# Two SBUF start addresses in a two-layer decoder kernel: the rows of y 192 bytes past a multiple of 256, the shared area 64 past one

## The chip, the core and the metric

The kernel runs on one NeuronCore of a Trainium2 chip, with the other cores idle. The metric is device time in microseconds (us). The reference's inputs and outputs are float32, and one launch computes the whole decoder trunk. SBUF is the on-chip memory that every operand of the compute engines is read from; an address here is the byte offset in each of its 128 partitions. TensorE is the matrix engine (PE in the profile, and PEld for its loads of the stationary operand), DVE is VectorE, ACT ScalarE, POOL GpSimd and SP the queue that issues the large DMAs.

## The reference, cut to what matters

```python
D_MODEL, SEQ, FFN_HIDDEN = 1024, 512, 2816
# layer 0
y = rmsnorm(x, g0)
cols = y @ w_in            # mLSTM heads and differential attention heads
x = x + concat(mlstm(cols), diff_attention(cols)) @ w_out
y = rmsnorm(x, g1)
x = x + (silu(y @ w_gate) * (y @ w_up)) @ w_down
# layer 1: the same, with native sparse attention (compressed, selected, window branches)
# then a final rmsnorm
```

Most of the arithmetic is in the products with weights: the input projections, the output projections, gate and up, and down.

## The kernel before, in words

Tokens stand in the free dimension (T = 512), features in the partitions, in KT = 8 tiles of 128. A weight unit is 8 tiles of 128x128 (11 for the down projection). SP loads each unit into one of four buffers `raw0` to `raw3` (L519). ACT copies it to `w_high`, rounded to float32r (L544), DVE writes the rest, raw minus high, to `w_low` (L563); both have two buffers. The activations are split likewise, into `y_high` and `y_low`, into `ffn_high` and `ffn_low` (the hidden rows of the FFN, 22 tiles), into `mix_high`/`mix_low` and into `o_high`/`o_low`. TensorE forms each product in three float32r matmuls, `mm3`, L672 to L674: high times high, high times low, low times high, each with a load of its own 128x128 stationary operand and, as a rule, 512 columns of the moving one.

```python
def mm3(o, ah, al, bh, bl, first, last):
    pe.matmul(o, ah, bh, start=first, stop=False)
    pe.matmul(o, ah, bl, start=False, stop=False)
    return pe.matmul(o, al, bh, start=False, stop=last)
```

`feature_unit` (L679) has the weights stationary and y moving; `token_unit` (L696) has y stationary and the weights moving. The down projection (`down_unit`) has the weights stationary and `ffn_high`/`ffn_low` moving; the output projections are of the same kind with the mixed or attention rows. `narrow_unit` makes the gate columns of layer 1 (stage GT): its stationary tiles are only 48 columns wide and lie 192 bytes apart, while in all other units the stationary tiles lie 512 bytes apart. `gate_unit` does the input and forget gates of layer 0. Between units of layer 0's projections, bursts of small float32 matmuls and transposes (L842 to L893) serve the attention heads and the mLSTM; the sets of layer 1's attention (L1148 transposed scores, L1228 transposes of probabilities, L1241 values) come in rounds of their own.

The order on every engine is written out by hand, with semaphores between engines; there is no scheduler. SBUF addresses are given by hand too. `place` (L335) hands out one tile after another from the running address `at[0]`, each rounded up to 32 bytes. The first tile, the constants, starts at 16512, which is 128 past a multiple of 256. Then come, in this order: the feature parameters, the residual `hT`, `y_high`, `y_low`, `rinv`, `raw0` to `raw3`, `w_high0`, `w_high1`, `w_low0`, `w_low1`, the four working tiles `work0` to `work3`, and small ones. Behind them begins the shared area, `arena` (L383): 44 rows of 2048 bytes, whose names (q, k, v, decay, `x_rows`, `ffn_high`, `mix_high`, `o_high`, scores and so on) are laid over one another as stages follow. `y_at` is where y begins; the transposed probabilities `probs_T`, `h_gained` and `out_rows` lie over y.

Starts of the tiles that matter, as bytes past a multiple of 256, from the sums of `place`:

| tiles | before |
|---|---|
| constants, residual | 128, 128 |
| y_high, y_low, rinv, raw, w_high, w_low (every buffer) | 128 |
| work0, work1, work2, work3 | 128, 160, 192, 224 |
| everything in the shared area that steps by whole rows | 128 |

The only lines of the placement that set these:

```python
hT = place("residual", KT * T)
y_at = at[0]
yh = place("y_high", KT * T, F32R)
...
arena = (at[0] + 127) // 128 * 128
```

Of the kernel before, what the change touches and what calls it, by code (L numbers as in the profile page):

```python
# [330 lines left out]
def trunk(nc, A, consts, out):  # L331
    with ExitStack() as ctx:
        at = [(nc.sbuf_base + 31) // 32 * 32]

        def place(name, width, dt=F32, offset=None):  # L335

            o = at[0] if offset is None else offset
            if offset is None:
                at[0] += (4 * width + 31) // 32 * 32
            return nc.alloc_sbuf_tensor_at(name, [P, width], dt, offset=o)[:, :]  # L340
# [9 lines left out]
        kc = place("shape_constants", K_END)  # L350
        par = place("feature_params", PROWS)
        hT = place("residual", KT * T)
        y_at = at[0]
        yh = place("y_high", KT * T, F32R)
        yl = place("y_low", KT * T, F32R)
# [24 lines left out]
        hid = place("cmp_hidden", 256)  # L380
        kcd = hid
        neghalf = place("neg_half", 32)
        arena = (at[0] + 127) // 128 * 128  # L383
        assert arena + 4 * 2 * HT * T <= nc.sbuf_usable_end, (arena + 4 * 2 * HT * T, nc.sbuf_usable_end)

        def row(name, first, rows, dt=F32):
# [2203 lines left out]
```

## Time and profile before

| what | us |
|---|---|
| three runs | 1353.18, 1356.54, 1356.42 |
| their median | 1356.42 |
| the profiled execution | 1355.16 |
| its span, first to last instruction | 1353.1 |
| TensorE busy in the span | 1325.5 (98%) |
| VectorE, ScalarE, GpSimd busy | 702.3, 554.6, 229.8 |

The profiled execution took 2.1 us more than its span, and 1.3 us less than the median of the runs. Busy shares of TensorE count a matmul until its results have drained, so consecutive matmuls overlap in it: what a matmul costs in a row of them is the distance from its start to the start of the next, not its duration. The timeline shows these starts; the table of stages shows how full TensorE is in each.

### The profile page before, as it was taken

Reading aid. Unit: us, or ns where it says so; the run is one execution under the profiler, and the core shown is the slowest. Engines: PE = TensorE matmul, PEld = TensorE weight load, DVE = VectorE, ACT = ScalarE, POOL = GpSimd, SP = SyncE. Lnnn points to the kernel's source line nnn. Section 1 sums busy time; section 2 is a strip of 40 time slices with the busy share of each in tenths; the row PEclk is TensorE's granted clock in tenths of the full one; section 3 lists DMA queues with packets and bytes.
Section 4 is the critical chain, followed back from the end, with each engine's and each line's share of the span. In section 5 each row is a group of like instructions: output and inputs, shape, how many; then the busy total and the mean of one; then the engine's idle time right before and its main releaser. Section 6 shows DMA issues by size and latency. Waiting matters only on the chain.

```text
span 1353.1 us, 17939 instructions
## 1 busy us (share of the span) xinstructions
PE 1325.5 (98%) x6396; PEld 1053.2 (78%) x6396; DVE 702.3 (52%) x1287; ACT 554.6 (41%) x1019; POOL 229.8 (17%) x233
## 2 busy tenths in 40 slices
PE   9999999999999999999999989998999999999997
PEld 7777688888888888888878855556888888888887
DVE  4479886543334333323798777685534333442222
ACT  5435665433333332222374457774433333332222
POOL 2047571221111111000000002112211111110000
PEclk9999999999999999999999999999999999999999
DMA  7321222333333344232344200000333333343311
GB/s 242 83 75 51 62 63 73 88 90 102 99 93 93 96 115 116 85 101 70 87 125 129 79 16 1 1 17 17 93 93 93 95 105 94 93 116 108 95 54 63
DMA packets 203944, 114.10 MB, mean 84 GB/s; under 512 B 5712, under 2 KB 200528, under 8 KB 203760
## 3 DMA queue, kind: packets, MB, share of 16 engines
q1 hardware_dynamic: 203264, 112.97, 28.8%
q0 software_dynamic: 416, 0.35, 0.3%
q8 instruction: 32, 0.52, 0.2%
q14 instruction: 24, 0.20, 0.0%
q10 hardware_dynamic: 208, 0.06, 0.0%
HBM read 111.27 MB, written 2.10 MB: 84 GB/s over the span
## 4 chain that ended last, share of the span: by engine, by line
PE 85%; DVE 6%; ACT 4%; issue 3%; POOL 1%; DVEq 0%; POOLq 0%; ACTq 0%
PE acc L672 24%; PE acc L674 24%; PE acc L673 24%; PE acc L1241 2%; PE aux L1148 1%; PE aux L1228 1%; ACT score L1679 1%; DVE w_low L563 1%; ACT w_high L544 1%; PE acc L1148 1%; PE acc L1130 1%; PE aux L1109 1%; PE aux L842 0%; PE aux L852 0%; ACT probs_T L592 0%
## 5 line engine op out<-in xcount | busy, mean ns | idle before, releaser
L563 DVE TENSOR_TENSOR w_low<-raw,w_high 128x1024 fp32r<-128x1024 f32 (+2 forms) x185 | 246.3, 1331 | 504.5 <-ACT w_high L544 504.5
L672 PE MATMUL acc<-y_high,w_high 128*128 128x512 f32 x992 | 392.1, 395 | 2.5 <-DVE w_low L555 2.0
L674 PE MATMUL acc<-y_high,w_low 128*128 128x512 f32 x992 | 386.8, 390 | 0.0
L673 PE MATMUL acc<-y_low,w_high 128*128 128x512 f32 x992 | 386.4, 389 | 0.0
L544 ACT ACTIVATE w_high<-raw 128x1024 fp32r<-128x1024 f32 (+2 forms) x186 | 205.7, 1106 | 311.0 <-PE acc L674 304.2
L672 PEld LDWEIGHTS acc<-y_high,w_high 128*128 128x128 f32 x992 | 185.8, 187 | 42.8 <-DVE w_low L555 3.4
L674 PEld LDWEIGHTS acc<-y_high,w_low 128*128 128x128 f32 x992 | 185.7, 187 | 40.1
L673 PEld LDWEIGHTS acc<-y_low,w_high 128*128 128x128 f32 x992 | 185.9, 187 | 38.8 <-issue 0.7
L672 PE MATMUL acc<-ffn_high,w_high 128*128 128x512 f32 (+1 forms) x374 | 141.0, 377 | 0.0
L673 PE MATMUL acc<-ffn_low,w_high 128*128 128x512 f32 (+1 forms) x374 | 140.9, 377 | 0.0
L674 PE MATMUL acc<-ffn_high,w_low 128*128 128x512 f32 (+1 forms) x374 | 140.9, 377 | 0.0
L2461 POOL TENSOR_TENSOR work<-work,work 128x512 f32<-128x512 f32 x44 | 56.9, 1293 | 417.7 <-DVE work L1749 417.7
L1514 ACT ACTIVATE ffn_high<-work 128x512 f32 (+1 forms) x44 | 27.8, 632 | 148.4 <-POOL work L2461 148.4
L1749 DVE TENSOR_TENSOR work<-acc,rinv 128x512 f32<-128x512 f32 x107 | 73.3, 685 | 17.1 <-PE acc L674 9.7
L1679 ACT ACTIVATE score<-score,neg_max 128x384 f32<-128x384 f32 (+3 forms) x128 | 68.7, 539 | 31.5 <-DVE neg_max L2326 31.5
L2447 POOL TENSOR_TENSOR work<-work,work 128x512 f32<-128x512 f32 x31 | 42.2, 1360 | 227.7 <-ACT work L1322 227.3
L673 PEld LDWEIGHTS acc<-ffn_low,w_high 128*128 128x128 f32 x374 | 70.4, 188 | 13.0
L672 PEld LDWEIGHTS acc<-ffn_high,w_high 128*128 128x128 f32 x374 | 70.4, 188 | 12.9
L674 PEld LDWEIGHTS acc<-ffn_high,w_low 128*128 128x128 f32 x374 | 70.4, 188 | 12.7
L2553 POOL TENSOR_TENSOR o_rows<-o_rows,work 128x512 f32<-128x512 f32 x16 | 20.3, 1270 | 258.1 <-DVE work L2348 258.1
L1509 ACT ACTIVATE work<-work 128x512 f32<-128x512 f32 x44 | 27.8, 633 | 80.3 <-DVE work L1749 80.3
L1315 ACT ACTIVATE y_high<-residual,feature_params 128x512 fp32r<-128x512 f32 x30 | 21.1, 722 | 49.6 <-DVE residual L1953 31.7
(336 smaller groups left out, 1705.7 us busy)
## 6 DMA issues: line engine op xcount, KB each, us to landing
raw<-in_l_w_in_dram SPq DMA_DIRECT2D x44, 512.0 KB, 3.8
raw<-in_l_w_gate_dram SPq DMA_DIRECT2D x44, 512.0 KB, 3.8
raw<-in_l_w_up_dram SPq DMA_DIRECT2D x44, 512.0 KB, 3.8
raw<-in_l_w_down_dram SPq DMA_DIRECT2D x32, 704.0 KB, 4.5
raw<-in_l_w_out_dram SPq DMA_DIRECT2D x16, 512.0 KB, 3.6
x_rows<-in_x_dram SPq DMA_DIRECT2D x4, 512.0 KB, 6.1
raw<-in_l_cmp_w_k_dram SPq DMA_DIRECT2D x4, 512.0 KB, 3.7
raw<-in_l_cmp_w_v_dram SPq DMA_DIRECT2D x4, 512.0 KB, 3.8
```

The costliest lines, as they stand in the source:

```text
L544: act.activation(dst, src, ACT.Copy).then_inc(S("split_high"), 1)
L563: dve.tensor_tensor(dst, src, high.bitcast(F32), ALU.subtract).then_inc(S("split_low"), 1)
L672: pe.matmul(o, ah, bh, start=first, stop=False)
L673: pe.matmul(o, ah, bl, start=False, stop=False)
L674: return pe.matmul(o, al, bh, start=False, stop=last)
L1148: pe.matmul(scores_at(n), qrot[a, q], k, start=True, stop=True).then_inc(S("s_scores"), 1)
L1509: act.activation(tmp[2 * (t % 2)][:, 0:T], tmp[2 * (t % 2)][:, 0:T], ACT.Silu)\
L1514: act.activation(Gh[:, tile_at(t, it, 2)], tmp[2 * (t % 2) + 1][:, 0:T], ACT.Copy)\
L1679: act.activation(probs_at(n), probs_at(n), ACT.Exp, scale=-1.0, bias=nmx[:, n % 16:n % 16 + 1], accum_out=rsum[:, n % 16:n % 16 + 1]).then ...
L1749: return dve.tensor_tensor(dst, ps(tile)[lo:hi, cols], rinv[lo:hi, cols], ALU.mult)
L2447: pool.tensor_tensor(tmp[0][:, 0:T], tmp[0][:, 0:T], tmp[1 + m % 2][:, 0:T], ALU.add)\
L2461: pool.tensor_tensor(up, tmp[2 * (t % 2)][:, 0:T], up, ALU.mult).then_inc(S("ffn_prod"), 1)
```

## The change

One line adds 64 bytes ahead of y. All that is placed behind it up to the shared area moves by 64 bytes. The start of the shared area is rounded in another way and moves from 138368 to 138560, by 192 bytes. Constants, parameters and residual stay.

```diff
@@ -350,6 +350,7 @@
         kc = place("shape_constants", K_END)
         par = place("feature_params", PROWS)
         hT = place("residual", KT * T)
+        at[0] += 64
         y_at = at[0]
         yh = place("y_high", KT * T, F32R)
         yl = place("y_low", KT * T, F32R)
@@ -380,7 +381,7 @@
         hid = place("cmp_hidden", 256)
         kcd = hid
         neghalf = place("neg_half", 32)
-        arena = (at[0] + 127) // 128 * 128
+        arena = (at[0] + 255) // 256 * 256 + 64
```

| tiles | before | after |
|---|---|---|
| constants, residual | 128 | 128 |
| y_high, y_low, rinv, raw, w_high, w_low | 128 | 192 |
| work0, work1, work2, work3 | 128, 160, 192, 224 | 192, 224, 0, 32 |
| the shared area | 128 | 64 |

Every engine executes the same instructions in the same order with the same waits; only addresses differ.

## Rows read from the trace of the kernel before

**Rows 1.** The page, busy time of TensorE, and its granted clock in 40 slices.
```profile
PE 1325.5 (98%) x6396; PEld 1053.2 (78%) x6396; DVE 702.3 (52%) x1287; ACT 554.6 (41%) x1019; POOL 229.8 (17%) x233
...
PEclk9999999999999999999999999999999999999999
```

**Rows 2.** Windows: stretch, length, busy us and count of each engine, clock, DMA.
```profile
290.00:550.00 260.00, 260.00 (x1149) 215.31 (x1148) 99.74 (x115) 82.39 (x95) 30.26 (x24) 1.00 0.34 100
...
985.00:1275.00 290.00, 290.00 (x1278) 239.72 (x1278) 108.12 (x122) 89.38 (x103) 33.86 (x27) 1.00 0.34 99
```

**Rows 3.** The chain that ended last, shares of the span by engine.
```profile
PE 85%; DVE 6%; ACT 4%; issue 3%; POOL 1%; DVEq 0%; POOLq 0%; ACTq 0%
```

**Rows 4.** Groups by line and form, TensorE: 512-column products; L673 and L674 alike.
```profile
L672 PE MATMUL acc<-y_high,w_high 128*128 128x512 f32 x984 | 389.0, 395 | 2.5 <-DVE w_low L555 2.0 <-DVE w_low L563 0.4
...
L672 PE MATMUL acc<-ffn_high,w_high 128*128 128x512 f32 x330 | 128.4, 389 | 0.0
L672 PE MATMUL acc<-w_high,y_high 128*128 128x512 f32 x96 | 40.1, 417 | 1.0 <-DVE y_low L1726 0.5 <-DVE w_low L563 0.2 <-DVE y_low L1766 0.2
...
L672 PE MATMUL acc<-o_high,w_high 128*128 128x512 f32 x56 | 22.4, 400 | 0.0
...
L672 PE MATMUL acc<-mix_high_d,w_high 128*128 128x512 f32 x32 | 12.6, 395 | 0.0
```

**Rows 5.** Timeline, TensorE, layer 0 gate/up: start us, duration; the second is 24 matmuls later.
```profile
399.66 0.39 PE L674 MATMUL acc<-y_high,w_low 128*128 128x512 f32 x1
...
405.10 0.39 PE L674 MATMUL acc<-y_high,w_low 128*128 128x512 f32 x1
```

**Rows 6.** Timeline, layer 1 down: 10 matmuls of 512 columns, then 10 of 256.
```profile
1321.70 0.39 PE L672 MATMUL acc<-ffn_high,w_high 128*128 128x512 f32 x1
...
1323.96 0.39 PE L673 MATMUL acc<-ffn_low,w_high 128*128 128x512 f32 x1
...
1342.00 0.28 PE L672 MATMUL acc<-ffn_high,w_high 128*128 128x256 f32 x1
...
1343.20 0.28 PE L673 MATMUL acc<-ffn_low,w_high 128*128 128x256 f32 x1
```

**Rows 7.** Timeline, layer 0 projections: first matmuls behind a burst; eleven from 172.57 to 175.11.
```profile
172.57 0.40 PE L673 MATMUL acc<-y_low,w_high 128*128 128x512 f32 x1
...
173.27 0.39 PE L673 MATMUL acc<-y_low,w_high 128*128 128x512 f32 x1
173.49 0.39 PE L674 MATMUL acc<-y_high,w_low 128*128 128x512 f32 x1
...
175.11 0.38 PE L852 MATMUL aux<-qk_m 128*128 128x128 f32 x2
```

**Rows 8.** Timeline, stage GT: 24 matmuls between the two starts.
```profile
742.58 0.40 PE L672 MATMUL acc<-y_high,w_high 128*48 128x512 f32 x1
...
748.14 0.33 PE L1109 MATMUL aux<-cmp_hidden,q_raw 128*128 128x64 f32 x2
```

**Rows 9.** Timeline of three transposes; then lines L1228, L763, L1241: ns min/median/max.
```profile
799.97 0.49 PE L1228 MATMUL aux<-shape_constants,score 128*128 128x128 f32 x3
L1228 PE MATMUL aux<-shape_constants,score x229: 272/273/333, 796.4 to 921.4; 128*128 128x128 f32 x115
L763 PE MATMUL aux<-work,shape_constants x8: 590/590/592, 29.1 to 990.7; 128*128 128x512 f32 x8
L1241 PE MATMUL acc<-probs_T,v_sel_win x152: 592/592/1062, 806.9 to 927.9; 128*64 128x512 f32 x152
```

**Rows 10.** Lines L1509 and L2461, the FFN's work tiles in turn: ns min/median/max.
```profile
L1509 ACT ACTIVATE work<-work x44: 631/633/634, 291.8 to 1218.2; 128x512 f32<-128x512 f32 x44
L2461 POOL TENSOR_TENSOR work<-work,work x44: 1282/1294/1297, 295.4 to 1223.7; 128x512 f32<-128x512 f32 x44
```

**Rows 11.** Waits: ScalarE's split of weights for TensorE: us, times, longest.
```profile
ACT w_high L544 <- PE acc L674: 304.2, 147, 6.4
```

**Rows 12.** The DMA queue that carries the loads: packets, MB, share.
```profile
q1 hardware_dynamic: 203264, 112.97, 28.8%
```

## The prediction

> **What bounds the kernel now.** I read the page first. TensorE is busy for 1325.5 of 1353.1 us at a granted clock of 0.9 or more in every slice, so at the upper of its two levels, 2.4 GHz [rows 1]. The windows by stage say where that is tight: the stretches of gate/up and down, one for each layer, are 100% TensorE, with VectorE at 37 or 38% and ScalarE at 31 or 32% beside it [rows 2]. The chain that ended last agrees, 85% of it on TensorE [rows 3]. So only what changes TensorE's own pace, or makes it wait, can change the time by much.
>
> The groups by form say what that pace is made of. High-times-high products with 512 columns number 984 with weights moving or stationary against y, 330 with the FFN's hidden rows, 96 more against y, 56 with `o_high`, and 32 each for the two halves of the mix (one is shown) [rows 4]. Each stands three times, as L672, L673 and L674: (984 + 330 + 96 + 56 + 64) x 3 = 4590, and some 50 in the gate stages and in auxiliary banks, 4640 in all. Of these (330 + 56 + 64) x 3 = 1350 read the shared area; the rest have y and weights as both operands.
>
> Their durations (389 ns and more) overlap. The timeline has the pace: in gate/up 24 matmuls take 405.10 - 399.66 = 5.44 us, **226.7 ns** each [rows 5]. In the last down tiles ten matmuls of 512 columns take 2.26 us (226 ns each, the same within rounding) and ten of 256 columns 1.20 us, 120 ns each [rows 6]. The difference, 106.7 ns for 256 columns, is one column per cycle at 2.4 GHz; what remains, 120 - 106.7 = **13.3 ns, is a fixed part of every such matmul**. 4640 x 13.3 = 62 us of the kernel hangs on that part. It is the largest thing that an address could touch.
>
> **The change part by part.** It removes, adds and reorders no instruction. Nothing is queued behind another thing than before, no wait is new. What is left is the duration of the same operations at other starts.
>
> ScalarE, GpSimd, VectorE. The trace already has one operation at different starts: in the FFN the work tiles alternate, `work0` or `work1` at 128 or 160 past a multiple of 256, `work2` or `work3` at 192 or 224. L1509 takes 631 to 634 ns over all 44, and L2461, which reads both kinds, 1282 to 1297 [rows 10]. A start worth 5% would split either into two groups. Cost zero. VectorE is taken to be the same, without such a row. All three stand beside TensorE: ScalarE waits 304.2 us in 147 places for TensorE to free the weight buffers [rows 11], so a few ns per operation would be hidden, except in the attention rounds of layer 1. If that cover were gone, VectorE at 702 us busy would pay 7 us for each per cent.
>
> DMA. The loads write runs of 512 bytes that now start 192 rather than 128 past a multiple of 256; either way a run lies across three stretches of 256 bytes. The queue is in use 28.8% of the time [rows 12]. Cost zero, hidden by TensorE's 100%.
>
> Float32 matmuls. L763 reads its moving operand from `work3`, 224 past a multiple of 256, and takes 590 ns. L1241 reads `probs_T`, 128 past one, and takes 592 ns for as many columns [rows 9]. These read a column in two cycles: L1228 with 128 columns takes 273 ns [rows 9], so a column is (592 - 273) / 384 = 0.83 ns. Cost zero.
>
> Float32r matmuls. Here no row shows a moving operand at another start than 128 past a multiple of 256, so the cost is bounded. Below: the whole fixed part goes, 13.3 ns x 4640 = -62 us. Above: the nearest row is stage GT, the only one whose stationary tiles step by 192 bytes and so begin 128, 64, 0 and 192 past a multiple of 256 in turn. Its 24 matmuls take 748.14 - 742.58 = 5.56 us, 231.7 ns each, 5.0 more than settled ones [rows 5, 8], and the unit before it ran without a break. For all 4640 that is +23 us. That row is mixed up with tiles of 48 columns, so it may not be the address at all.
>
> Which value? Rows 7 speak for zero. Behind each burst the pace is not settled: the eleven matmuls from 172.57 to 175.11 take 2.54 us, 231 ns each, and one of them takes 0.22 us, less than settled. Those all have starts 128 past a multiple of 256. So **the 5 ns can come with no change of start at all**; the pace finds its settled value within about ten matmuls, and in the long stages stays there, although the stationary tile walks through eight places 512 bytes apart and the moving row goes from y to the shared area [rows 2, 5, 6]. I take 0 ns for matmuls with both operands in the part that moves by 64 bytes, since those keep their distance to one another, and 0 for the 1350 whose operands now begin 192 and 64 past a multiple of 256, with less confidence.
>
> Sum: 1355.2 us, the profiled execution, plus 0. The median of the runs shown is 1.3 us above it, and a median is what is compared, so the forecast is **1356 us**.
>
> The Trainium skill speaks for no effect at one place: TensorE: Matmul & The Clock Gate, section Part 2: What happens when you issue a matmul, says that TensorE reads the moving and the stationary operand through two independent ports, so that loading the next weights takes nothing from the running matmul. By that the distance between the two starts could not count. The trace does not bear it out fully, since identical matmuls follow one another after 231 ns on average behind a burst, and one after 0.22 us [rows 7].
>
> **The rivals.** (1) The fixed part is a cost of the start. The transposes of L1228, three in 0.49 us at 273 ns each, follow one another after (490 - 273) / 2 = 109 ns [rows 9], where 128 columns at two cycles need 106.7: a fixed part of 2.3 ns, not 13.3. If float32r, which reads twice as fast, pays the other 11 ns for beginning in the middle of a stretch of 256 bytes, and 64 or 192 spares it, 4640 x 11 = 51 us go: 1305 us. For it: the fixed part is the same in every stage, as are the starts. Against it: the shortest step of a matmul with one column per cycle, 0.22 us [rows 7], still has 7 ns over its 213, and 192 is no rounder than 128. Chance 0.14.
> By the same page of the Trainium skill, section Back-to-back issue gap, 512 columns take 518 cycles, 215.8 ns. The trace does not agree, with 226.7; if the starts were what keeps the two apart, the page too gives a gain of 51 us.
>
> (2) The same in part: the two streams get in each other's way when they begin at the same place in a stretch of 256 bytes, and only the 1350 matmuls on the shared area are taken apart by the change (weights at 192, rows at 64). 1350 x 11 = 15 us less: 1341 us. A settled pace of 224 ns, near the short step of rows 7, on all of them would give about the same, 4640 x 2.7 = 12.5 us. Chance 0.19.
>
> (3) Slower, in the shared area. The settled pace of 226.7 is a balance between the loads of stationary tiles and the moving rows. With starts 128 bytes apart the balance is not found in down and output projections, and they keep the unsettled 231.7: 1350 x 5.0 = 6.8 us more, 1363 us. The point from which it decides is 4.1 us, 3 ns for each of these. Chance 0.12.
>
> (4) The same everywhere, because the start of the moving row alone decides: 4640 x 5.0 = 23 us, 1379 us. Chance 0.13.
>
> (5) That the change does not do what it says is excluded by the sums of addresses; that it does it and nothing on the chip minds is the forecast, 0.42.
>
> **How the numbers follow.** A difference of 0.3%, 4.1 us, is about what a measurement of this kernel can tell from none, given runs from 1353.2 to 1356.5. No change: 0.42, with its own range 1352 to 1360. Faster: rivals 1 and 2, 0.33. Slower: rivals 3 and 4, 0.25. The range goes from 1305, the price of rival 1, to 1379, that of rival 4. The bounds lie further out, 1293 below, and 1379 is no strict end above, so that about half of those two rivals' chance, 0.13, is left outside, and some uncertainty of the cases themselves.
>
> **What would show it.** If I am right: 24 matmuls of gate/up again 5.44 us apart, ten of down again 2.26, transient steps of 0.22 to 0.24 us behind bursts as before, and ScalarE and GpSimd durations within 1%. Rival 1 shows a pace near 216 in gate/up and down, rival 2 in down only; rival 3 has 230 or more in down alone, rival 4 in both. In all four the number of TensorE's records in 290 to 550 us moves with it: now 1149. I am wrong outright if the durations of VectorE's or ScalarE's operations move and the attention rounds change length while the pace of rows 5 stands.

## The result, and the profile after

The changed kernel takes 1361.24 us (median of 6 runs, 1360.49 to 1364.85), the kernel before 1355.18 us (6 runs, 1352.88 to 1356.54). The ratio is 1.0054, with a 95% interval of 1.0037 to 1.0071: 5 to 10 us slower, with 7.3 us in the middle. The forecast was no effect, 1356 us with 1352 to 1360 as its own range, and it was wrong; the time lies inside the wide range only because of the rivals, of which the third had the place and 1363 us.

The page of the changed kernel. All line numbers of the program are one higher than before.

```profile
span 1357.7 us, 17939 instructions
...
PE 1328.5 (98%) x6396; PEld 1050.3 (77%) x6396; DVE 702.0 (52%) x1287; ACT 554.8 (41%) x1019; POOL 229.8 (17%) x233
```

Nothing but TensorE has moved [rows 1]: VectorE 702.0 against 702.3 us, ScalarE 554.8 against 554.6, GpSimd 229.8 twice. The q1 loads take 28.7% of their queue against 28.8% [rows 12]. The operations that the prediction watched, ScalarE's and GpSimd's on the work tiles, whose starts all changed, and the wait of ScalarE for TensorE (min/median/max in ns; then the view of waits):

```profile
L1510 ACT ACTIVATE work<-work x44: 631/632/633, 290.7 to 1219.8; 128x512 f32<-128x512 f32 x44
L2462 POOL TENSOR_TENSOR work<-work,work x44: 1282/1296/1302, 294.3 to 1225.3; 128x512 f32<-128x512 f32 x44
ACT w_high L545 <- PE acc L675: 310.8, 148, 6.6
```

They stand where they stood [rows 10, 11]. So do the float32 matmuls of rows 9: L764 takes 592 ns with its moving operand now at 32, where it took 590 at 224, and L1242 592 at 192 as before at 128. Now the timeline of TensorE, for three pairs of starts that are 24 matmuls apart: layer 0's output projection, layer 0's gate/up, layer 0's down.

```profile
259.86 0.39 PE L673 MATMUL acc<-mix_high_m,w_high 128*128 128x512 f32 x1
...
265.43 0.40 PE L673 MATMUL acc<-mix_high_m,w_high 128*128 128x512 f32 x1
...
399.49 0.39 PE L673 MATMUL acc<-y_high,w_high 128*128 128x512 f32 x1
...
404.93 0.39 PE L673 MATMUL acc<-y_high,w_high 128*128 128x512 f32 x1
...
559.58 0.40 PE L675 MATMUL acc<-ffn_high,w_low 128*128 128x512 f32 x1
...
565.18 0.40 PE L675 MATMUL acc<-ffn_high,w_low 128*128 128x512 f32 x1
```

Gate/up takes 5.44 us for 24, 226.7 ns each, as before [rows 5], although y and the weights both moved. Down takes 5.60 us, **233.3 ns** each, and the output projection 5.57 us, 232.1; before, 24 matmuls of the output projection took 5.44 (259.99 to 265.43), and the same 24 of down as well:

```profile
559.46 0.39 PE L674 MATMUL acc<-ffn_high,w_low 128*128 128x512 f32 x1
...
564.90 0.39 PE L674 MATMUL acc<-ffn_high,w_low 128*128 128x512 f32 x1
```

The same shows in a count. The windows (length, then busy us and count of PE, PEld, DVE, ACT, POOL, then clock, DMA share, GB/s) hold, from 525 to 635 us of down, 487 matmuls before and 473 after, 2.9% fewer:

```profile
525.00:635.00 110.00, 110.00 (x487) 91.11 (x486) 33.46 (x29) 29.11 (x29) 10.07 (x8) 1.00 0.31 87
```

```profile
525.00:635.00 110.00, 110.00 (x473) 88.46 (x473) 33.27 (x29) 29.12 (x29) 10.08 (x8) 1.00 0.30 85
```

The count that the prediction named as the sign, TensorE's records from 290 to 550 us, went from 1149 to 1144; gate/up kept its pace, and the loss is from the first part of down, which begins at 518 us.

So the price is 330 x 3 = 990 matmuls of down at 6.7 ns and 360 of the output projections at 5.4 ns, an estimate of 6.6 + 1.9 = 8.5 us. That lies within the interval of the runs. The trace bears out the larger term: from the first matmul of gate/up to the last of down, layer 0 takes 348.38 us before and 351.89 after, layer 1 337.48 and 340.52 (without the last, narrower tiles), 6.55 us more in the two. The two profiled spans differ by 4.6 us only, since each has its own stretches at the lower clock. From 60 to 80 us the kernel before had a mean granted clock of 0.91 and did 71 matmuls, the changed one 1.00 and 79, which is worth about 1.7 us; from 850 to 940 us too it was the kernel before whose clock was lower (0.96 and 0.98 against 1.00), and from 775 to 812 us the changed one (0.95 against 1.00). Whole runs compared at one mean clock agree with the estimate: at 0.997 three runs of the changed kernel have a mean span of 1359.3 us, and eight of the kernel before, taken with the experiments, 1351.6.

### The profile page after: what moved, and what is told of

Its sections match the earlier page's. It is cut to its first block, busy times and chain, and to the rows that moved or that the text cites. A ratio compares the mean times of both kernels' runs of the same rounds, so it can differ in the third digit from the quotient of the medians.

```text
span 1357.7 us, 17939 instructions
## 1 busy us (share of the span) xinstructions
PE 1328.5 (98%) x6396; PEld 1050.3 (77%) x6396; DVE 702.0 (52%) x1287; ACT 554.8 (41%) x1019; POOL 229.8 (17%) x233
## 3 DMA queue, kind: packets, MB, share of 16 engines
q1 hardware_dynamic: 203264, 112.97, 28.7%
## 4 chain that ended last, share of the span: by engine, by line
PE 86%; DVE 6%; ACT 3%; issue 3%; DMA 0%; POOL 0%; SPq 0%; DVEq 0%; POOLq 0%; ACTq 0%
PE acc L673 25%; PE acc L675 24%; PE acc L674 24%; PE acc L1242 2%; PE aux L1149 1%; PE aux L1229 1%; DVE w_low L564 1%; ACT score L1680 1%; PE acc L1149 1%; PE aux L853 1%; ACT w_high L545 1%; PE acc L1131 1%; PE aux L1110 1%; DMA x_rows<-in_x_dram 0%; PE aux L843 0%
## 5 line engine op out<-in xcount | busy, mean ns | idle before, releaser
L673 PE MATMUL acc<-y_high,w_high 128*128 128x512 f32 x992 | 391.7, 395 | 2.5 <-DVE w_low L556 1.9
L674 PE MATMUL acc<-y_low,w_high 128*128 128x512 f32 x992 | 386.2, 389 | 0.0
L673 PEld LDWEIGHTS acc<-y_high,w_high 128*128 128x128 f32 x992 | 185.8, 187 | 42.8 <-DVE w_low L556 3.3
L674 PEld LDWEIGHTS acc<-y_low,w_high 128*128 128x128 f32 x992 | 185.8, 187 | 38.5 <-issue 0.7
L673 PE MATMUL acc<-ffn_high,w_high 128*128 128x512 f32 (+1 forms) x374 | 142.9, 382 | 0.0
L674 PE MATMUL acc<-ffn_low,w_high 128*128 128x512 f32 (+1 forms) x374 | 142.7, 382 | 0.0
L674 PEld LDWEIGHTS acc<-ffn_low,w_high 128*128 128x128 f32 x374 | 70.2, 188 | 15.1
L673 PEld LDWEIGHTS acc<-ffn_high,w_high 128*128 128x128 f32 x374 | 70.2, 188 | 15.1
L2448 POOL TENSOR_TENSOR work<-work,work 128x512 f32<-128x512 f32 x31 | 42.2, 1361 | 234.2 <-ACT work L1323 233.7
```

The costliest lines, as they stand in the source:

```text
L2448: pool.tensor_tensor(tmp[0][:, 0:T], tmp[0][:, 0:T], tmp[1 + m % 2][:, 0:T], ALU.add)\
```

## The experiments

Two theories could explain a slower down projection beside an unmoved gate/up. A: the distance between the starts of the stationary and the moving operand decides. It stayed 0 in gate/up and became 128 bytes (modulo 256) in down. B: the start of the moving row alone decides, and 64 past a multiple of 256 is a bad one.

### A bench of starts

A kernel of its own, whose only work is this loop; `tile` cuts a float32r region that is filled from x.

```python
for n, (_, s, m, w, pitch) in enumerate(CASES):
    o = bank[n % 4][0:w, :]
    for i in range(72):
        k, j = i // 3 % 8, i % 3
        left = tile(st_at + (6144 if j == 2 else 0) + s + k * pitch, w)
        right = tile(mv_at + (18432 if j == 1 else 0) + m + 2048 * k, 512)
        pe.matmul(o, left, right, start=(i % 24 == 0), stop=(i % 24 == 23))
```

> Leaves out the whole trunk and measures one thing: rows of float32r matmuls, 72 without a break for each of 26 cases, in the pattern of the kernel (128 stationary columns, 512 moving ones, high-high, high-low, low-high). Cases 1 to 16 keep the stationary tiles 128 past a multiple of 512 and move the start of the moving rows by 0, 32, ... 480 bytes against them. Cases 17 to 20 have both at 0, 64, 192 and 320. Cases 21 to 23 have them 128 bytes apart, the stationary ones at 0, 64 and 192. Cases 24 to 26: 48 stationary columns, 512 bytes and 192 bytes apart, then the first case again. Theory A (the distance between the two starts decides, as rival 3 has it): cases 1, 17 to 20 and 26 settle at 226.7 ns, 72 in 16.3 us; case 5 (distance 128) and 21 to 23 take 233.3 ns, 16.8 us, all alike. Theory B (the start of the moving row alone decides, 64 past a multiple of 256 being a bad one): case 15 or whichever begins at 64 takes 16.8 us, and so does the pair at 64 and 64 (case 18), while case 5 need not. Theory C (layer stages, other engines beside it): every case 226.7, 16.3 us.

The timeline merges the matmuls of a case into one row, 72 in each (start, us until the last has drained, what). The time of a case is the start of the next row less its own. The first ten cases are distances 0, 32, ... 288:

```profile
21.58 18.35 PE L64 MATMUL bank_a<-filled 128*128 128x512 f32 x72 [21.58 <-ACT filled L53]
39.77 16.97 PE L64 MATMUL bank_b<-filled 128*128 128x512 f32 x72
56.58 16.65 PE L64 MATMUL bank_c<-filled 128*128 128x512 f32 x72
73.07 16.97 PE L64 MATMUL bank_d<-filled 128*128 128x512 f32 x72
89.88 16.96 PE L64 MATMUL bank_a<-filled 128*128 128x512 f32 x72
106.68 17.03 PE L64 MATMUL bank_b<-filled 128*128 128x512 f32 x72
...
157.14 16.51 PE L64 MATMUL bank_a<-filled 128*128 128x512 f32 x72
173.49 16.97 PE L64 MATMUL bank_b<-filled 128*128 128x512 f32 x72
...
290.86 16.52 PE L64 MATMUL bank_a<-filled 128*128 128x512 f32 x72
307.22 16.53 PE L64 MATMUL bank_b<-filled 128*128 128x512 f32 x72
...
356.24 16.89 PE L64 MATMUL bank_a<-filled 128*128 128x512 f32 x72
372.97 16.95 PE L64 MATMUL bank_b<-filled 128*128 128x512 f32 x72
...
406.49 17.12 PE L64 MATMUL bank_d<-filled 128*48 128x512 f32 x72
423.45 16.78 PE L64 MATMUL bank_a<-filled 128*48 128x512 f32 x72
440.07 16.49 PE L64 MATMUL bank_b<-filled 128*128 128x512 f32 x72
```

The first case holds the start at the lower clock: the trace has its first matmuls 427 ns apart. Distance 32 takes 56.58 - 39.77 = 16.81 us, 233.5 ns each; distance 64 takes 16.49, **229.0**; 96 and 128 take 16.81 and 16.80, 233.5 and 233.3; 160 takes 234.2; distance 256, from 157.14, takes 16.35, 227.1, like distance 0. Case 17, both at 0, takes 16.36 us (290.86 to 307.22), and the other pairs of equal starts the same. Case 21, stationary at 0 and moving at 128, takes 16.73, 232.4 (356.24 to 372.97), with no operand at 64. This is theory A, with a period of 256 bytes, and all distances from 256 to 480 repeat those from 0 to 224. It was not quite right that all pairs 128 bytes apart are alike: with the stationary start at 0, 64, 128 and 192 they take 232.4, 233.2, 233.3 and 232.4. Theory C, which needs other engines beside TensorE, falls as well: none works here, and the cases still differ.

The bench also shows what stage GT was: 48 stationary columns at a pitch of 512 bytes take 423.45 - 406.49 = 16.96 us, 235.6 ns, and at 192 bytes 16.62, 230.8. The narrow tile is off 226.7 even where every start is alike; walking through other starts in steps of 192 bytes made it 4.8 ns faster, not slower.

The trace has each single step too. In case 17 the first ones are 230, 233, 236, 224, 231, 236, 228, 232 and 231 ns, and then 227, 227, 226 to the end of the row; behind the burst of rows 7 they were 235, 233, 236, 224, 231, 236, 228, 233, 231, 226. So a row at distance 0 needs some nine matmuls to settle with nothing else running. At distance 128 it settles too, into one of two other sequences: steps of 229 and 238 ns in turn (case 5, 233.3 on average) or steps of 228 to 241 ns (case 21, 232.4). Down in the changed kernel has the first, the output projections the second, and both have their starts at 192 and 64. So the 0.9 ns between the two need not come from the place of the pair; what picks the sequence is not shown.

### The changed kernel with the distance put back

```diff
-        arena = (at[0] + 255) // 256 * 256 + 64
+        arena = 138432
```

> The changed kernel, but with the shared area at 138432, 192 past a multiple of 256 like y and the weights. Theory A: distance 0 again everywhere, down and output projections return to 226.7 ns, about 8.9 us less than the changed kernel in these stages: 1353 to 1356 us, the time of before. Theory B: 192 is a start at which y has kept its pace, so the same. It tells A and B from a theory in which the move of the weights and working tiles by 64 bytes costs by itself (then about 1361 us).

Ratio to before 1.0017, interval 1.0003 to 1.0031; median 1356.25 us. Two starts in down, 24 matmuls apart:

```profile
559.54 0.39 PE L675 MATMUL acc<-ffn_low,w_high 128*128 128x512 f32 x1
...
564.99 0.39 PE L675 MATMUL acc<-ffn_low,w_high 128*128 128x512 f32 x1
```

5.45 us, 227 ns. Moving y, weights and work tiles by 64 bytes therefore does not cost what the change costs. Of the 0.4 to 4 us that remain, the trace shows nothing in the long stages: gate/up and down together take 348.38 us in layer 0 and 337.48 in layer 1, to the hundredth as before. The clock accounts for most of it. The twelve runs of this kernel had a mean granted clock of 0.9950, the 17 of the kernel before beside them 0.9965, and among those 17 the span goes from 1348.2 us at 0.999 to 1354.5 at 0.993, about 1.05 us per 0.001. That is an estimate of 1.6 us out of 2.0 between the mean spans. Whether the placement has a part in the lower clock isn't shown.

### The shared area alone, 128 and 192 bytes from the weights

Both are the kernel before with one line changed:

```diff
-        arena = (at[0] + 127) // 128 * 128
+        arena = 138496      # 138560 in the second
```

> The kernel before with the shared area alone moved, to 138496, a multiple of 256; y and weights stay 128 past one. The distance is 128 bytes as in the changed kernel, with no operand at 64 or 192. Theory A: 233.3 ns in down and output projections, 1361 to 1365 us. Theory B: no moving row begins at 64, so no cost, 1355 us, unless 0 is a bad start too.

Ratio 1.0074, interval 1.0054 to 1.0095. Down in its timeline:

```profile
559.45 0.40 PE L673 MATMUL acc<-ffn_high,w_high 128*128 128x512 f32 x1
...
565.05 0.40 PE L673 MATMUL acc<-ffn_high,w_high 128*128 128x512 f32 x1
```

5.60 us, 233.3 ns, with moving rows on a multiple of 256. Theory B would have had to call 0 a bad start as well.

> The kernel before with the shared area alone moved, to 138560, 64 past a multiple of 256 as in the changed kernel; y and weights stay at 128, the distance is 192 bytes. Theory B: the moving rows begin where those of the changed kernel do, so 233.3 ns and about 1364 us. Theory A: the pace of distance 192, which the bench gives as case 7; it need not be 233.3. Either way the y stages stay at 226.7.

Ratio 1.0071, interval 1.0053 to 1.0088, and the same 5.60 us in down (559.54 to 565.14). The bench had 233.5 for distance 192 (16.81 us for its case 7). This run alone does not part the theories, as both allow it.

### Does the price follow the distance?

> The kernel before with the shared area alone moved by 256 bytes, to 138624. Theory A with a period of 256: distance 0, pace 226.7 in down, time of before, 1353 to 1357 us. If only the exact place counted, or the space left between the small tiles and the area, it would cost as the other moves did, 1363 us.

`arena = 138624`: ratio 1.0002, interval 0.9986 to 1.0017, down at 5.44 us for 24. A move by 256 bytes is free.

> The kernel before with the shared area alone at 138432, 192 past a multiple of 256: 64 bytes from the weights. Theory A with the bench's price: 229.0 ns in down and output projections, 2.3 ns x 1350 = 3.1 us more, about 1357 to 1359 us. Theory B (the start of the moving row alone): 192 was free with y and weights there, so no cost.

`arena = 138432` with y and weights left at 128: ratio 1.0031, interval 1.0015 to 1.0046, that is 2 to 6 us where 3.1 were expected. Down:

```profile
559.47 0.39 PE L674 MATMUL acc<-ffn_low,w_high 128*128 128x512 f32 x1
...
564.97 0.39 PE L674 MATMUL acc<-ffn_low,w_high 128*128 128x512 f32 x1
```

5.50 us, 229.2 ns, as in the bench. The same absolute start as in the kernel that put the distance back cost nothing there, at distance 0. That is what theory B cannot have.

```diff
         rinv = place("rinv", T)
+        at[0] += 64
         raw = [place(f"raw{s}", UNIT) for s in range(RAW)]
...
-        arena = (at[0] + 127) // 128 * 128
+        arena = 138432
```

> The kernel before with 64 bytes put between rinv and the raw weights, and the shared area at 138432: weights and area 192 past a multiple of 256, y at 128. The area's 1350 matmuls keep distance 0, the 3290 of y get 192 (feature units) or 64 (token units, roles swapped, about 290 of them with y stationary in all). Theory A: y stages at 233.3 ns, 6.7 ns x 3000 = 20 us more and 0.7 us for token units, 1373 to 1378 us, down at 226.7. Theory B: no change, since 128 and 192 are both free starts for moving rows.

Ratio 1.0127, interval 1.0107 to 1.0147: 17 us (14 to 20), median 1371.61 us, where the expectation had 1373 to 1378; theory B had no change. Its gate/up, 24 apart, and its down, ten apart:

```profile
399.17 0.40 PE L675 MATMUL acc<-y_low,w_high 128*128 128x512 f32 x1
...
404.77 0.40 PE L675 MATMUL acc<-y_low,w_high 128*128 128x512 f32 x1
...
559.68 0.39 PE L674 MATMUL acc<-ffn_high,w_high 128*128 128x512 f32 x1
...
561.94 0.39 PE L675 MATMUL acc<-ffn_low,w_high 128*128 128x512 f32 x1
```

Now gate/up is at 233.3 and down at 226, the mirror image of the change. The expectation charged every matmul of y with 6.7 ns. By the trace only the two gate/up stages pay it, 6.67 us each; the projections of layer 1 take 1.6 us more (111.31 and 112.88), and all that stands before layer 0's output projection 0.5 us. Layer 0's projections come some eleven at a time between bursts and had not settled before either [rows 7]: a row of ten steps behind a burst, from 173.39 to 175.72, takes 233 ns each here, against 231 before. They had 2 ns to lose, not 6.7.

### Is there a better placement?

The cases of the bench were replaced: moving starts 4 to 248 bytes off, and each of the four operands (stationary high, stationary low, moving high, moving low) on its own.

> Leaves out the whole trunk; 72 float32r matmuls without a break for each of 79 cases, as in the first bench. Cases 1 and 2: all four starts (stationary high and low, moving high and low) alike. Cases 3 to 15: the moving starts 4, 8, 12, 16, 24, 48, 60, 64, 68, 80, 224, 240 and 248 bytes past the stationary ones. Cases 16 to 79: the stationary high and low and the moving low each at 0, 64, 128 or 192 against the moving high. Theory A (the distance decides, modulo 256): case 10 (64) at 229.0 ns as before, 72 in 16.5 us; the others either at 233.3, 16.8 us, or, if a distance counts by whole runs of 64 or 32 bytes, the first seven of them at 226.7, 16.3 us. In the last 64 only those with all four alike are at 16.3. If some mixed case lies below 16.3 us, there is a placement that beats the kernel before.

Rows of cases 2 to 5 (distances 0, 4, 8, 12) and of case 16, all four alike again:

```profile
38.60 16.48 PE L63 MATMUL bank_b<-filled 128*128 128x512 f32 x72
54.92 17.30 PE L63 MATMUL bank_c<-filled 128*128 128x512 f32 x72
72.06 16.90 PE L63 MATMUL bank_d<-filled 128*128 128x512 f32 x72
88.79 16.64 PE L63 MATMUL bank_a<-filled 128*128 128x512 f32 x72
105.27 16.83 PE L63 MATMUL bank_b<-filled 128*128 128x512 f32 x72
...
272.54 16.52 PE L63 MATMUL bank_d<-filled 128*128 128x512 f32 x72
288.90 16.86 PE L63 MATMUL bank_a<-filled 128*128 128x512 f32 x72
```

Case 2 takes 16.32 us, 226.7 ns. Four bytes of distance take 17.14 us, 238.1 ns; 8 bytes 232.4; 12 bytes 228.9; a distance does not count in runs of 32 or 64 bytes. The expectation had 233.3 or 226.7 for all distances but 64; the thirteen that were tried lie between 228.7 (60 bytes) and 239.6 (68 bytes). Of the 64 combinations only the one with all four alike, 16.36 us, is below 228; the next is 228.7 (16.47 us), most lie at 231 to 233.5. No case of either bench with 512 columns beats 226.7, so there was no placement to try against the kernel before.

### With how many columns does the distance count?

> Leaves out the whole trunk; 72 matmuls without a break for each case. Case 1 repeats the reference. Cases 2 to 11: 512, 448, 384, 320 and 256 moving columns, each at distance 0 and at 128 bytes from the stationary start. Cases 12 to 17: 96, 64 and 32 stationary columns with 512 moving ones, at 0 and 128. Cases 18 and 19: float32 instead of float32r, at 0 and 128. Case 20: the reference again. Theory D (a fixed part per matmul, as the prediction read it: 13.3 ns at distance 0, 20 ns at 128): 512, 448, 384, 320 columns at 226.7, 200, 173.3, 146.7 ns, and 6.7 more at distance 128. Theory E (part of the loss grows with the columns, and at 256 columns something else, the load of the stationary tile, sets 120 ns): fewer columns lose less than 13.3 ns, and at 256 both distances stand at 120, as the changed kernel's last tile does. Float32 at two cycles a column: no difference between 0 and 128. Narrower stationary tiles: if the loads disturb the moving rows, the price of the distance shrinks with their width; the 48-column case of the first bench speaks against that.

Rows of cases 2 to 7, 10 to 13, and one behind each group (stationary columns behind the *, moving columns behind the x of 128x512):

```profile
40.43 16.48 PE L66 MATMUL bank_b<-filled 128*128 128x512 f32 x72
56.75 16.95 PE L66 MATMUL bank_c<-filled 128*128 128x512 f32 x72
73.54 15.03 PE L66 MATMUL bank_d<-filled 128*128 128x448 f32 x72
88.41 14.84 PE L66 MATMUL bank_a<-filled 128*128 128x448 f32 x72
103.08 12.65 PE L66 MATMUL bank_b<-filled 128*128 128x384 f32 x72
115.57 12.84 PE L66 MATMUL bank_c<-filled 128*128 128x384 f32 x72
128.25 10.72 PE L66 MATMUL bank_d<-filled 128*128 128x320 f32 x72
...
149.37 8.79 PE L66 MATMUL bank_b<-filled 128*128 128x256 f32 x72
158.00 8.71 PE L66 MATMUL bank_c<-filled 128*128 128x256 f32 x72
166.54 16.72 PE L66 MATMUL bank_d<-filled 128*96 128x512 f32 x72
183.10 16.85 PE L66 MATMUL bank_a<-filled 128*96 128x512 f32 x72
199.79 16.72 PE L66 MATMUL bank_b<-filled 128*64 128x512 f32 x72
```

In ns per matmul, distance 0 and 128: 512 columns 226.7 and 233.2; 448 columns 206.5 and 203.8; 384 columns 173.5 and 176.1; 320 columns 146.7 twice; 256 columns 119.9 and 118.6. With 96 stationary columns 230.0 and 231.8; with 64 and 32 they stand at 229 to 231.5, at either distance. Neither theory of the expectation holds. The 13.3 ns over one cycle a column is there at 512, 384, 320 and 256, but it is 20 ns at 448, and the price of the distance is anything from +6.5 to -2.7 ns. Float32 took 858 and 853 ns, no loss at 128. In the trace each of these float32 matmuls is two records, 429 ns apart at either distance, so a column costs two cycles in a record and four in all; the expectation, and the prediction in its words on float32, have the two of a record. What is shown of 226.7 ns is this: with 512 moving columns only full tiles of 128 columns at distance 0 have it. Other distances give 228.7 to 239.6, narrower tiles 229 to 235.6.

## Why the prediction was wrong

**The step that failed** is the value taken for float32r matmuls: "0 for the 1350 whose operands now begin 192 and 64 past a multiple of 256, with less confidence". They cost 6.7 ns each in down and 5.4 in the output projections, 8.5 us. The other half of that step, 0 for matmuls whose operands keep their distance, was right: gate/up at 226.7, and the kernel with the distance put back.

**Why it failed.** Two facts were in hand and weighed wrongly. The prediction took from the unsettled steps behind bursts that a loss can come with no change of start, and let that speak for zero. They showed rather that 226.7 is reached only after some nine matmuls, with 231 on the way [rows 7]; the right question was whether it would still be reached from other starts. And the walk of stationary tiles in steps of 512 bytes was read as a sign that starts don't count, where 512 is two of the periods.

**Rival 3** was nearest: it had the place (down and output projections), the cause (starts 128 bytes apart), the settled pace lost there and kept in gate/up. Its size was short: 5.0 ns, giving 6.8 us, where 6.7 and 5.4 ns were measured. The 5.0 came from stage GT, whose tiles of 48 columns take 235.6 ns even at a pitch of 512 bytes and distance 0. That the two figures were near was luck. Nor do these stages keep an unsettled pace, as it had it: they settle into sequences of their own, down into 229 and 238 ns in turn. The balance of loads and moving rows that it names as the reason is not shown. Rival 3 was given 0.12, too little. Rivals 1 and 2 fell: distance 0 is the best place, not the worst, and nothing lies below 226.7. Rival 4 fell with gate/up, which kept 226.7 at a new start, and with theory B.

**What held:** TensorE bounds and nothing else counts; ScalarE, GpSimd and DMA lost nothing at other starts; VectorE, taken without a row, neither (702.0 us). Float32 matmuls do not mind. Reading a fixed part of 13.3 ns in every float32r matmul was right for the two row lengths it was read from, at distance 0, and is no general law, by the bench of sizes.

On the two places of the Trainium skill. Page TensorE: Matmul & The Clock Gate, section Part 2: What happens when you issue a matmul, has the load of the next stationary tile on a read port of its own, taking no bandwidth from the running matmul. The prediction drew from it that the distance between the two starts could not count, and there the runs differ: it moves the pace by 6.7 ns, 3%, with full tiles of float32r. Whether the ports are where that happens, no run shows. Its section Back-to-back issue gap has 518 cycles, 215.8 ns, for 512 columns in an isolated matmul; no case of the three benches with float32r and 512 columns reached it, and the lowest was 226.7.

**Still open:** why. The runs show that the loss depends on the distance modulo 256, on the width of the tile and on the length of the row, and it does not rise or fall steadily with any of them. That two streams of reads collide in SBUF would fit a distance, but not that 448 columns gain by 128 bytes; it is argued, not shown. Open too is what sets the granted clock of a run, on which the last 2 us of such comparisons hang.

## What to carry to other kernels

In a kernel bound by float32r matmuls of 128 x 128 x 512, put the stationary and the moving operands, high and low parts alike, at the same place modulo 256 bytes, and check that an added small tile between them does not undo it: 64 bytes in the wrong place cost 17 us of 1355, a shared area 128 or 192 bytes off cost about 10. The sign counts: moving rows 64 bytes past the stationary tiles cost 2.3 ns each, 64 bytes short of them (192 past) 6.7. The runs had stationary tiles 512 bytes apart; other steps were not tried with full tiles. Where the time per matmul in a long row is shorter than behind its gaps, it is a settled pace that an edit can lose; starts 24 matmuls apart show it in two lines where durations (0.39 and 0.40 us) hardly do. A bench with one case per row, compared at equal clock, finds such a thing in one run.

## What the runs showed of the hardware

- The issue pace of float32r matmuls (128 stationary and 512 moving columns, 2.4 GHz) depends on the distance between the operands' starts, modulo 256 bytes: 226.7 ns at 0, 229.0 at 64, 233.3 to 233.5 at 32, 96, 128 and 192, 238.1 at 4. The absolute start does not count at distance 0, where 0, 64, 128, 192 and 320 gave 226.7 to 227.2; pairs 128 bytes apart at four places took 232.4 to 233.3.
- At distance 0 the pace of 226.7 ns is reached after some nine matmuls of 224 to 236 ns, in the bench as in the kernel; at distance 128 the steps stay at 229 and 238 in turn, or run from 228 to 241 with a mean of 232.4.
- Narrow stationary tiles are slower, not faster: 48 columns take 235.6 ns, 96, 64 and 32 columns 229 to 232, where 128 take 226.7, all with 512 moving columns at 2.4 GHz.
- A row of 448 columns takes 206.5 ns, 20 over one cycle a column, where 512, 384, 320 and 256 have about 13.3 over it.
- A float32 matmul of 128 stationary and 512 moving columns is two records 429 ns apart and takes 853 to 858 ns; the distance between the starts, 0 or 128, does not change that.
